# The first mixer's start and the order of work ahead of the experts in a two-block fp32 kernel

## The reference, cut to what matters

```
# first block, start
h = x * rsqrt(mean(x*x) + eps) * norm_mix_g
p, q, k, v = split(h @ w_in)            # 1024 -> 4 x 512
q, k = rope(q), rope(k)                 # rotation by position
... pooling of p, differential attention of q, k, v, output projection,
... feed-forward block with a depthwise convolution

# second block
... input projection, SSD mixer, mLSTM mixer, output projection
h2 = x * rsqrt(mean(x*x) + eps) * norm2_w
group = top1(h2 @ wg + bg); experts = top2 of the 8 in that group
y = sum over the 2 experts of gate * (silu(h2 @ w_gate) * (h2 @ w_up)) @ w_down
out = rmsnorm(x + y) * norm_f_w
```

## Time and profile before

| | |
|---|---|
| median of 3 runs | 1109.15 us |
| profiled execution | 1107.42 us, span 1105.6 us |
| granted TensorE clock, mean | 0.989 |
| PE busy, in 40 slices (tenths) | 5999999999999989889988879999999999999997 |
| DVE busy, in 40 slices | 4765677666667656777666769999999999999987 |
| ACT busy, in 40 slices | 4553755555455645556422657777777777777764 |
| moved by the transfers | 253.61 MB, mean 229 GB/s |
| loads of experts' gate weights | 52, two a unit |

### The profile page before, as it was taken

One profiled execution on the slowest core, in us unless ns is written; L12 is line 12 of the kernel. 1 busy time (PEld: TensorE's weight loads), 2 busy tenths in 40 slices (PEclk: granted clock), 3 DMA queues, 4 the chain that ended last, 5 costly groups with the idle time before them and its releaser, 6 DMA issues.

```text
span 1105.6 us, 15082 instructions
## 1 busy us (share of the span) xinstructions
PE 1048.0 (95%) x5682; PEld 890.0 (80%) x5682; DVE 842.0 (76%) x1075; ACT 663.0 (60%) x797; POOL 33.3 (3%) x40
## 2 busy tenths in 40 slices
PE   5999999999999889989888879999999999999997
PEld 5878999999999777889777867787877878778785
DVE  4765677666667656777666769999999999999987
ACT  4553755555455645556422657777777777777764
POOL 0000000000010100100020000000000000000000
PEclk9999999999999999999999989999999999999999
DMA  9634356465525444233301768999989989899881
GB/s 337 242 115 133 115 191 202 159 211 187 156 85 173 137 150 148 81 115 121 108 31 41 267 207 327 375 353 366 387 352 369 370 353 390 352 365 378 351 333 42
DMA packets 82711, 253.61 MB, mean 229 GB/s; under 512 B 4161, under 2 KB 42177, under 8 KB 62657
## 3 DMA queue, kind: packets, MB, share of 16 engines
q1 hardware_dynamic: 81808, 251.27, 61.2%
q10 hardware_dynamic: 816, 1.23, 0.4%
HBM read 251.44 MB, written 1.05 MB: 228 GB/s over the span
## 4 chain that ended last, share of the span: by engine, by line
PE 77%; DVE 10%; ACT 7%; issue 4%; POOL 1%; DMA 1%; DVEq 0%; SPq 0%; POOLq 0%; ACTq 0%
PE bank L1745 21%; PE bank L1747 21%; PE bank L1746 21%; PE bank L2212 4%; ACT WH L502 4%; DVE WL L943 4%; PE bank L2164 1%; DVE CV L1178 1%; PE bank L2194 1%; POOL sm L1705 1%; DMA cn<-in_cn 1%; PE bank L1751 1%; PE bank L1771 1%; ACT CV L509 1%; ACT CV L675 0%
## 5 line engine op out<-in xcount | busy, mean ns | idle before, releaser
L943 DVE TENSOR_TENSOR WL<-raw,WH 128x2048 fp32r<-128x2048 f32 (+1 forms) x235 | 504.7, 2178 | 112.3 <-ACT WH L502 112.3
L502 ACT ACTIVATE WH<-raw 128x2048 fp32r<-128x2048 f32 (+1 forms) x235 | 427.1, 1824 | 104.7 <-PE bank L1747 88.7
L1745 PE MATMUL bank<-WH,MXH 128*128 128x512 f32 x552 | 219.9, 398 | 3.7 <-DVE MXL L1619 2.3
L1747 PE MATMUL bank<-WH,MXL 128*128 128x512 f32 x552 | 216.5, 392 | 0.0
L1746 PE MATMUL bank<-WL,MXH 128*128 128x512 f32 x552 | 216.2, 392 | 0.0
L1745 PE MATMUL bank<-HTH,WH 128*128 128x256 f32 x576 | 165.7, 288 | 3.5 <-DVE CV L1178 2.6
L1747 PE MATMUL bank<-HTH,WL 128*128 128x256 f32 x576 | 163.6, 284 | 0.0
L1746 PE MATMUL bank<-HTL,WH 128*128 128x256 f32 x576 | 163.6, 284 | 0.0
L1745 PE MATMUL bank<-WH,HTH 128*128 128x512 f32 x348 | 138.0, 396 | 4.9 <-DVE HTL L960 2.4
L1746 PE MATMUL bank<-WL,HTH 128*128 128x512 f32 x348 | 135.6, 390 | 0.0
L1745 PEld LDWEIGHTS bank<-WH,MXH 128*128 128x128 f32 x552 | 104.8, 190 | 25.3 <-DVE MXL L1619 2.7
(11 more groups left out here) (366 smaller groups left out, 1118.2 us busy)
## 6 DMA issues: line engine op xcount, KB each, us to landing
raw<-in_exp_w_gate SPq DMA_DIRECT2D x52, 1024.0 KB, 8.3
raw<-in_exp_w_up SPq DMA_DIRECT2D x52, 1024.0 KB, 7.8
raw<-in_exp_w_down SPq DMA_DIRECT2D x52, 1024.0 KB, 5.7
raw<-in_w_in SPq DMA_DIRECT2D x34, 1024.0 KB, 5.3
raw<-in_w_up SPq DMA_DIRECT2D x22, 1024.0 KB, 5.4
raw<-in_w_down SPq DMA_DIRECT2D x11, 1024.0 KB, 5.4
raw<-in_w_out SPq DMA_DIRECT2D x8, 1024.0 KB, 5.1
raw<-in_w_o SPq DMA_DIRECT2D x4, 1024.0 KB, 5.5
```

The lines of the kernel that those rows point to most:

```text
L502: e.activation(WH[i % HL][:, 0:n], raw[i % RAW][:, 0:n], ACT.Copy).then_inc(a_wh, 1)
L943: e.tensor_tensor(l, r, h.bitcast(F32), ALU.subtract).then_inc(v_wl, 1)
L1745: e.matmul(out_, ah, bh, start=start, stop=False)
L1747: return e.matmul(out_, al, bh, start=False, stop=stop)
```

## The change

- SP issues `cn` ahead of X, and the three loads that ACT issued (`br`, `pool_a`, `pool_w`) are issued by SP between pieces.
- PE transposes the rows of X itself as each tile lands. The factor of the norm is applied later: as a scalar in the first two instructions of `rope`, and as ACT's scale in the evictions of v and p. The row copies (`row0`, `row1`) go. The filler is 18 products in place of 26.
- Piece 0 is split in two halves of 1024 columns, each with its own semaphore, between the evictions of column pairs 0, 1 and 2, 3. Split 2 comes ahead of the angles.
- `H2H` and `H2L` are written with their columns in the order in which the gathering reads them, so that its weights are contiguous. ACT and DVE read X at every eighth element in exchange.
- The gates' product on PE stands between the gate and the up half of unit 0. The transposes of `SEL` come after unit 0 in other PSUM banks, and `turn_hidden(0)` no longer waits for their copies; the down product does.
- On DVE the gates' arithmetic comes ahead of splits `NP + 2` and `NP + 3`; unit 1's low features come ahead of `gate_hidden(0)`; of the register loads only the code of unit 0 stands ahead of `gate_column(0)`. On ACT unit 1's high features come ahead of split `NP + 3`, and split `NP + 5` ahead of the copies of the transposed selection.

```diff
@@ sync
-            for t in range(T):
-                e.dma_start(X[:, t, :], ...).then_inc(d_x[t], 16)
             e.dma_start(cn[:, 0:n0], a["cn"][:, 0:n0]).then_inc(d_cn, 16)
+            for t in range(T):
+                e.dma_start(X[:, t, :], ...).then_inc(d_x[t], 16)
             e.dma_start(pt[:, :], a["pt"]).then_inc(d_pt, 16)
+            load_pieces(0, 2)
             e.dma_start(sm[:, 0:2].bitcast(I32), a["positions"]).then_inc(d_pos, 16)
-            load_pieces(0, 2)
+            load_pieces(2, 3)
+            e.dma_start(br[:, :], ...).then_inc(d_br, 16)
+            load_pieces(3, 5)
             e.dma_start(cn[:, n0:NCN], a["cn"][:, n0:NCN]).then_inc(d_cn2, 16)
-            load_pieces(2, 18)
+            load_pieces(5, 7)
+            e.dma_start(pool_a, a["pool_a"]).then_inc(d_pa, 16)
+            e.dma_start(pool_w, ...).then_inc(d_pw, 16)
+            load_pieces(7, 18)
@@ scalar, start
-            squares("mix", d_x, (16, 16))
-            row1("mix")
+            square("mix", 0, d_x[0], 16)
             e.wait_ge(d_pt, 16)
-            columns("mix", "norm_mix_g", 0, (4, 5, 6, 7), HTH)
-            split(0)
+            columns("mix", "norm_mix_g", 0, (4, 5, 6, 7), HTH, (0, 1))
+            square("mix", 1, d_x[1], 16)
+            e.wait_ge(d_raw[0], 16)
+            e.activation(WH[0][:, 0:PC // 2], raw[0][:, 0:PC // 2], ACT.Copy).then_inc(a_w0, 1)
+            e.activation(WH[0][:, PC // 2:PC], raw[0][:, PC // 2:PC], ACT.Copy).then_inc(a_wh, 1)
+            columns("mix", "norm_mix_g", 0, (4, 5, 6, 7), HTH, (2, 3))
             split(1)
+            split(2)
             for i, dst in enumerate((sin, cos)):
...
-            for i in range(2, 4):
-                split(i)
+            split(3)
@@ vector, start
-            row0("mix")
-            columns("mix", "norm_mix_g", 0, (4, 5, 6, 7), HTH, HTL)
-            split(0)
+            e.wait_ge(d_pt, 16)
+            columns("mix", ..., (0, 1))
+            e.wait_ge(a_w0, 1)
+            e.tensor_tensor(WL[0][:, 0:PC // 2], ..., ALU.subtract).then_inc(v_w0, 1)
+            e.wait_ge(a_wh, 1)
+            e.tensor_tensor(WL[0][:, PC // 2:PC], ..., ALU.subtract).then_inc(v_wl, 1)
+            columns("mix", ..., (2, 3))
+            means("mix")
             split(1)
+            split(2)
@@ rope
-                e.tensor_tensor(A, src, cb, ALU.mult).then_inc(own.up(), 1)
-                e.tensor_tensor(B, src, sbb, ALU.mult).then_inc(v_ropm, 1)
+                e.wait_ge(g_rstd, RSTD["mix", t])
+                e.scalar_tensor_tensor(out=A, in0=src, scalar=rs[:, t:t + 1], in1=cb, op0=ALU.mult,
+                                       op1=ALU.mult).then_inc(own.up(), 1)
+                e.scalar_tensor_tensor(out=B, in0=src, scalar=rs[:, t:t + 1], in1=sbb, ...)
@@ tensor, start
-            norm_columns("mix", (4, 5, 6, 7))
-            warm(26, 0)
+            columns(X, (4, 5, 6, 7), ((d_x[0], 16), (d_x[1], 16)))
+            warm(18, 0)
@@ H2 (scalar; the vector engine's H2L likewise)
+        def by_row(v):
+            return v.rearrange("q (p k) -> q k p", k=8)
+        def in_rows(v):
+            return v.rearrange("q (k p) -> q k p", k=8)
-                m = e.activation(H2H[:, t, :], X[:, t, :], ACT.Copy, scale=rs[:, t:t + 1])
+                m = e.activation(in_rows(H2H[:, t, :]), by_row(X[:, t, :]), ACT.Copy, scale=rs[:, t:t + 1])
@@ gathering on PE
-                            m = e.matmul(bank[GATB[k]][:, 0:NS // 2], part[:, t, k:D:8], SEL[:, t, hs],
+                            m = e.matmul(bank[GATB[k]][:, 0:NS // 2], part[:, t, k * 128:(k + 1) * 128], SEL[:, t, hs],
@@ scalar, ahead of the experts
             load_tile(1)
+            e.wait_ge(v_xst, 4)
+            e.wait_ge(a_xst, 12)
+            features(1)
             split(NP + 3)
...
             split(NP + 4)
+            split(NP + 5)
             for j in range(3):
...
-            split(NP + 5)
@@ vector, ahead of the experts
-            split(NP + 2)
-            split(NP + 3)
             e.wait_ge(a_route, A_ROUTE["dm"])
...
-            split(NP + 4)
+            split(NP + 2)
+            split(NP + 3)
...
-            load_tile(0)
-            gate_column(0)
-            gate_hidden(0)
-            split(NP + 5)
-            load_tile(1)
+            load_code(0)
+            gate_column(0)
+            split(NP + 4)
+            load_tile(1)
+            features_low(1)
+            gate_hidden(0)
+            split(NP + 5)
+            tile[0] = 0
+            load_code(1)
+            count = e.value_load(TBI[0:1, 3:4], min_val=0, max_val=UNITS)
@@ tensor, unit(0)
                     elif u == 0:
+                        gate_matrix()
                         e.wait_ge(a_xst, 10)
@@ tensor, after unit(0)
-            gate_matrix()
+            turn_selection()      # waits v_gm, banks 7, 5, 6 in place of 7, 4, 5
```

More of the change, by code:

```diff
@@ L129 @@
 GATB = [7, 0, 1, 2, 3, 4, 5, 6]
+SELB = [7, 5, 6]
 SB = [[5, 4], [6, 7]]
@@ L502, in split, with square @@
                 e.activation(WH[i % HL][:, 0:n], raw[i % RAW][:, 0:n], ACT.Copy).then_inc(a_wh, 1)
+            def square(name, t, sem_x, x0):
+                e.wait_ge(sem_x, x0)
+                if SQ[name, t] > 1:
+                    e.wait_ge(a_sq, SQ[name, t] - 1)
+                e.activation(cvf, X[:, t, :], ACT.Square, accum_out=ss[:, t:t + 1]).then_inc(a_sq, 1)
             def squares(name, sem_x, x0):
                 for t in range(T):
[L506 to L509, removed]
+                    square(name, t, sem_x[t], x0[t])
             def row1(name):
@@ L513, in row1, with columns @@
                 e.activation(H[:, 1, :], X[:, 1, :], ACT.Copy, scale=rs[:, 1:2]).then_inc(a_h1, 1)
-            def columns(name, gname, k0, banks, dh):
+            def columns(name, gname, k0, banks, dh, part=None):
                 for j, w in enumerate(banks):
+                    if part and j not in part:
+                        continue
                     e.wait_ge(p_cols, COL[name, j])
@@ L596, in scalar @@
                 evac("v", t, PI["v", 1])
-                e.activation(VV[:, t, 0:512], bank[t][:, :], ACT.Copy).then_inc(a_vcp, 1)
+                e.wait_ge(g_rstd, RSTD["mix", t])
+                e.activation(VV[:, t, 0:512], bank[t][:, :], ACT.Copy, scale=rs[:, t:t + 1]).then_inc(a_vcp, 1)
             probs_T(0)
@@ L605, in scalar @@
                 evac("p", t, PI["p", 1])
-                e.activation(VV[:, t, 512:1024], bank[2 + t][:, :], ACT.Copy).then_inc(a_pcp, 1)
+                e.activation(VV[:, t, 512:1024], bank[2 + t][:, :], ACT.Copy, scale=rs[:, t:t + 1]).then_inc(a_pcp, 1)
             mean_copy(0)
@@ L851, in load_tile, with features @@
                 tile[u] = e.value_load(TBI[u:u + 1, 1:2], min_val=0, max_val=NT - 1)
+            def features(u):
+                for i in range(2):
+                    xs4 = XST[i].rearrange("p k (t c) -> p k t c", t=NT)
+                    e.activation(XCH[u % 2][:, 4 * i:4 * i + 4, :].unsqueeze(2), xs4[:, :, bass.ds(tile[u], 1), :],
+                                 ACT.Copy).then_inc(a_xch, 1)
             load_tile(1)
+            e.wait_ge(v_xst, 4)
+            e.wait_ge(a_xst, 12)
+            features(1)
             split(NP + 3)
@@ L861, in scalar @@
                 e.activation(SELT[:, 2 * j:2 * j + n // 2, :].rearrange("p a b -> p (a b)"),
-                             bank[(7, 4, 5)[j]][:, 0:128 * n], ACT.Copy).then_inc(a_selT, 1)
-            split(NP + 5)
+                             bank[SELB[j]][:, 0:128 * n], ACT.Copy).then_inc(a_selT, 1)
             def turn_hidden(u):
@@ L876, in unit @@
                     e.wait_ge(p_used, unit_base(u - 2) + 4)
[L877 to L883, removed]
+                    features(u)
                 i = unit_base(u)
@@ L951, in row0, with columns @@
                     mean_eps(rs[:, t:t + 1], ss[:, t:t + 1], D).then_inc(v_ms, 1)
+            def row0(name):
+                means(name)
                 e.wait_ge(g_rstd, RSTD[name, 0])
                 e.tensor_scalar(H[:, 0, :], X[:, 0, :], rs[:, 0:1], None, ALU.mult).then_inc(v_h0, 1)
-            def columns(name, gname, k0, banks, dh, dl):
+            def columns(name, gname, k0, banks, dh, dl, part=None):
                 for j, w in enumerate(banks):
+                    if part and j not in part:
+                        continue
                     e.wait_ge(a_colh, 2 * COL[name, j])
@@ L1437, in vector @@
             for t in range(T):
-                m = e.scalar_tensor_tensor(out=H2L[:, t, :], in0=X[:, t, :], scalar=rs[:, t:t + 1],
-                                           in1=H2H[:, t, :].bitcast(F32), op0=ALU.mult, op1=ALU.subtract)
+                m = e.scalar_tensor_tensor(out=in_rows(H2L[:, t, :]), in0=by_row(X[:, t, :]), scalar=rs[:, t:t + 1],
+                                           in1=in_rows(H2H[:, t, :].bitcast(F32)), op0=ALU.mult, op1=ALU.subtract)
             m.then_inc(v_route, 1)
```

64 lines of the change are left out of this document (38 added, 26 removed).

## The result

The changed kernel took 1092.66 us (median of 4 runs, 1090.41 to 1093.3) beside 1110.3 for the kernel before on the same chip: ratio 0.984, 95% interval 0.9815 to 0.9863. The forecast was 1092.0, the range 1086 to 1099. The profiled execution took 1093.04 (span 1091.2), against 1107.42 (1105.6): 14.4 less, where the terms made 16.9.

The account below looks back on a forecast made before the run. PE is busy for 95% of the span, so only a sooner start or fewer PE holes help. 7.3 + 9.6 = 16.9 off 1107.42 gives 1090.5; with 1.7 for the median, 1092 us, range 1086 to 1099.

Parts of the forecast that it names:

- part 1: The start: first projection product 8.7 us sooner, less 1.4, gives 7.3 us (4.5 to 9).
- part 2: Ahead of the experts: 8.5 us to unit 1, plus 1.6 for clock, less 0.5, gives 9.6 (5 to 12).
- Landings and first product: At the start: X0 lands at 5.0, transposes end at 8.8, first projection product at 13.4, 8.7 us sooner.
- The stall at the second turn: At `turn_qk(1)`: PE newly waits 1.3 us (0 to 2.5) for VectorE's rotation of k.
- The selection products: In the routing: 64 products with contiguous weights take 10.8 us, the first 12 at half clock; end 5.2 sooner.
- The strided accesses: Writing H2: VectorE's pair reading X at every eighth float costs 0.7 us more, bounds 0 to 1.4.
- The hole ahead of unit 1: PE's idle stretch before the second expert unit: 1.9 us, where 6.6 stood before.
- Full clock at unit 1: Second expert unit starts at full clock, not 0.50: 8 products at 0.23 in place of 0.43 save 1.6 us.
- the first (half of part 2): Ahead of the experts: strides cost 1.4, the hole grows 2.5, the clock falls again: 1097 us; chance 0.17.
- The second: At the start: VectorE or landings bind, so part 1 gives only 4 us: 1095.5 us; chance 0.13.
- The third: At the start, X0 lands at 6.6 as before, part 1 under 6; if both parts fail, 1109 us, chance 0.04.
- The fourth (a slower loop): In the expert loop of 26 units: each unit grows; 1.0 us a unit gives 1118 us; chance 0.04.

Follow-up runs that it names:

- e2: Only the part of the change ahead of the experts, on the start of the kernel before: 1099.45 us, ratio 0.9917.
- e8: The changed kernel with 12 filler products in place of 18 at the start: 1091.74 us, ratio 0.9832.
- e9: The changed kernel itself measured once more, nothing altered: 1090.87 us, ratio 0.9832.
- e6: The changed kernel with 58 in place of 36 filler products ahead of the selection products: 1091.28 us, ratio 0.9833.
- e12: The changed kernel with e10 and e11 together, and 48 in place of 36 fillers ahead of the selection products: 1088.61 us, ratio 0.9809.
- e3: The changed kernel with H2 in the old order of columns, so the selection's weights are strided again: 1096.29 us, ratio 0.9874.
- e4: The changed kernel with the old order of loads, X ahead of `cn` and three loads on ScalarE's queue: 1096.83 us, ratio 0.9898.
- e7: The changed kernel with H2's new column order made by strided writes in place of strided reads: 1092.35 us, ratio 0.9831.
- e10: The changed kernel with 12 fillers at the start and the rotation of k ahead of v's second split on VectorE: 1092.72 us, ratio 0.9847.
- e11: The changed kernel with the first 128 rows of H2 written early, while PE makes the logits: 1090.38 us, ratio 0.9823.
- e5: The changed kernel with H2's low part moved off VectorE: ScalarE writes scaled rows, GpSimd subtracts; 1092.35 us, ratio 0.9831.
- e1: Only the start of the change, with routing and experts of the kernel before: 1101.03 us, ratio 0.9933.

## Why the prediction was right

The terms were read from waits and lists, and the two parts came near the sums: part 1 8.06 at the sum into X (7.3 forecast), part 2 8.1 to unit 1 and 1.7 behind it in e2, together 9.8 (9.6 forecast). That the sums fit so well is luck in part: single terms were off by 0.4 to 1.5 us, and these errors mostly cancel. In part 1 the first product came 0.4 later than forecast and the stall was 1.1 shorter; in part 2 the products (0.9) and the strides (0.9) cost more than forecast, the hole ahead of unit 1 (1.45) and split 6 (0.5) less. By step:

- *Landings and first product.* X0 at 5.0 (5.0), transposes to 8.69 (8.8), first product 13.76 (13.4): the fillers took 5.07, not 4.5. The forecast took one mean, 0.126, but the fillers have two paces: an instruction lasts 421 ns up to a certain moment, as the 16 transposes ahead of them do, and 275 ns behind it. The moment lies near 10.5 us in the changed kernel, near 8.7 in e8, 9.2 in e9, and 16.9 in the kernel before. The granted clock is shown as 1.00 throughout, but the ratio is near that of the clock's two levels, and the four hidden transposes that began unit 1 at half clock before lasted 435 ns each. That the start runs at the lower level is argued from this and not shown; what sets the moment stays open.
- *The stall at the second turn.* Forecast 1.3, seen 0.17 (0.2 to 0.6 in e6 to e9). The vector list ran to 42.17 against a forecast 43.3: the rotation took 4.56 and not 5.0 (4.75 and 0.25 for the factor), since the idle time of 0.54 that it had inside before is not there, and it began 0.7 sooner (37.61 against 38.3). The factor in the rotation costs 0.07 an instruction. This is the mis-sized term that made part 1 0.8 better.
- *The selection products.* Forecast 10.8, seen 11.7: 18 at half clock and not 12, and the matrix came later against the end of the fillers (wait of 4.9, before 3.3). With a wait of 0.25 in e12, and none in e6, none of them ran at 0.50.
- *The strided accesses.* Forecast 0.7, bounds 0 to 1.4, seen 1.59 (4.06 - 2.47). The upper bound was wrong: the weight load's pace through such columns is no upper bound for VectorE. One element costs 4.06 / 2048 = 1.98 ns, before 1.21; on ScalarE 2.05 and 1.06. The Trainium skill (SBUF — State Buffer, Specifications) asks for two hits on a 16-byte line; every eighth fp32 has one, and the trace agrees. It gives no price; the rows here do.
- *The hole ahead of unit 1.* Forecast 1.9, seen 0.45. From the end of the selection products to the gated hidden values VectorE needed 14.8 (618.35 to 633.19) where the forecast had 16.3 (622.1 to 638.4); the tile load and the low part of unit 1 took 1.2 of it and not 2.0. The late split 6, forecast at 0.5, made no wait of PE in unit 1.
- *Full clock at unit 1.* Forecast 1.6. From unit 1 to the end of the span it is 455.6, 455.5 and 455.5 in e2, e3 and e4 against 457.3 before, so 1.7 to 1.8. The changed kernel shows 457.2 and in e9 456.4: its last units lose most of it again, 1.2 in the first profile in waits (1.8 and 0.7 where e2 has 1.3 and none), 0.5 in e9. e7 and e10 to e12 have the same loop and take 455.4 to 455.6, so this loss too comes with the execution and not with the kernel.
- *Not forecast.* These losses in the last units, and 1.6 to 1.8 us of half clock in the second block's mixers, in the first profile only. The median of the kernel before also lies 1.7 above its profiled execution, so both medians may hold some of it, and the difference of the medians, 17.6, lies near the 17.9 of the two parts.

Of the rivals, the first (half of part 2) had its 0.7 for the strides, but not the hole nor the clock. The second is disproved by 8.06, though its mechanism is there: in e8 1.3 us on PE's side brought 0.17 at the sum into X. The third is disproved too: X was there at 5.0, and the products came 0.147 apart. The fourth (a slower loop) is disproved: unit 1 to the end takes 457.2 and 456.4 in the two profiles, 457.3 before.

## What to carry to other kernels

Put first in the queue the one small load that everything waits for (here `cn`, 102 KB), and keep loads that are not yet needed from running beside it: 6.1 of the 17.6 us came from the two together, by an estimate mostly from the second. When data is laid out anew for one reader, price the access that does it on the engine that does it, with contiguous and strided rows of that engine; here 1.6 of 4.1 us went back into the chain. And before a step is given to an idle GpSimd, look at what VectorE does beside it. Last, when two profiles are compared over a short stretch, first see that the granted clock was the same in both; e11 against e9 shows 1.3 us that are not there against e10.

## What the runs showed of the hardware

- While GpSimd ran two instructions of 2.33 us, VectorE's small ones took 1.95 and 2.27 in place of 0.19 and 0.20 (e5).
- A stride costs on ScalarE about the same in a write (3.94 for two of 1024 columns) as in a read (4.20), contiguous 2.17.
- At 0 to 4 places between 365 and 446 us the granted clock fell to 0.50, in some executions of a kernel and not in others. In the first profile of the changed kernel each fall came shortly behind an idle stretch of PE of 0.86 to 2.57 us; in e9 idle stretches of 0.82 to 2.53 at like places had no fall behind them.
- With one engine issuing, `cn` and X first, the transfers moved 323 GB/s from 2 to 6 us (e1 too); with ScalarE's loads beside them 204, and 206 in e4.
- At the start one 128x128 instruction of PE lasted 421 ns and later 275, with a granted clock shown as 1.00 for both; the step lay between 8.7 and 16.9 us, at a different place in every profile read for it.
